# Four reorderings in a two-block transformer kernel on one core: copies before exps, one subtraction on another engine, one transpose later, one wait later

## The reference, cut to what matters

```python
mem_n = rms_norm(mem, mem_norm)
for i in range(2):
    hn = rms_norm(h, norm_pre[i])
    k_m, v_m = split(mem_n @ w_mem_kv[i])              # keys and values of the memory
    if i == 0:   # latent attention: q, k, v made from a 672-wide latent, with rope
        proj = hn @ w_in_a;  main = mla_mixer(...)     # 12 heads, causal softmax
    else:        # attention with cumulated forget gates added to the logits
        proj = hn @ w_in_b;  main = fox_mixer(...)     # 12 heads, causal softmax
    mem_out = memory_attention(q_m, k_m, v_m)          # 4 heads, softmax over 256 memory tokens
    y = concat([main, mem_out]) * silu(gate)
    h = h + rms_norm(y @ w_out[i], norm_post[i])
```

## Time and profile before

| what | value |
|---|---|
| three runs | 1202.85, 1203.97, 1208.3 us |
| profiled execution, its own time | 1202.74 us |
| span of its instructions | 1201.0 us |
| PE busy | 1179.9 us (98%) |
| ACT, DVE, POOL busy | 594.2, 534.2, 432.5 us |
| mean granted PE clock | 0.994 of full |

### The profile page before, as it was taken

The page is one execution under the profiler, slowest core; times in us unless marked ns, Lnnn a source line. Parts: engine busy times, 40 slices in busy tenths (PEclk is TensorE's granted clock), DMA queues, the critical chain, the costliest instruction groups (busy, mean ns, idle before and its releaser), DMA issues.

```text
span 1201.0 us, 16232 instructions
## 1 busy us (share of the span) xinstructions
PE 1179.9 (98%) x6127; PEld 915.8 (76%) x6127; DVE 534.2 (44%) x979; ACT 594.2 (49%) x1246; POOL 432.5 (36%) x261
## 2 busy tenths in 40 slices
PE   7999999999999999989999999999999999999998
PEld 7988855568988666658888987787666677888886
DVE  4211465644210555553476645601786760033333
ACT  7344666554343655564644654544565552333142
POOL 6534721214344222215344322344222223444451
PEclk9999999989999999989999999999999999999999
DMA  8533211202336999813222321233121213323221
GB/s 297 141 106 68 64 23 47 68 21 84 108 98 77 95 62 79 122 35 90 89 88 68 108 67 57 75 101 105 53 58 52 67 37 91 102 92 102 96 97 70
DMA packets 111550, 100.97 MB, mean 84 GB/s; under 512 B 21157, under 2 KB 98289, under 8 KB 111473
## 3 DMA queue, kind: packets, MB, share of 16 engines
q1 hardware_dynamic: 108928, 95.35, 33.8%
q0 software_dynamic: 864, 3.15, 0.7%
q10 hardware_dynamic: 1680, 1.44, 0.4%
HBM read 94.68 MB, written 2.10 MB: 81 GB/s over the span
## 4 chain that ended last, share of the span: by engine, by line
PE 94%; DVE 2%; ACT 2%; DMA 1%; issue 1%; POOL 1%; SPq 0%; DVEq 0%; ACTq 0%
PE bank L592 49%; PE bank L1936 8%; PE bank L1629 7%; PE bank L1423 6%; PE bank L861 4%; PE bank L879 3%; PE bank L895 3%; PE bank L1952 2%; PE bank L1250 2%; PE bank L1967 2%; PE bank L1979 2%; PE bank L865 1%; PE bank L1718 1%; DMA w_raw<-in_w_mem_kv 1%; PE bank L702 1%
## 5 line engine op out<-in xcount | busy, mean ns | idle before, releaser
L527 POOL TENSOR_TENSOR w_lo<-w_raw,w_hi 128x1024 fp32r<-128x1024 f32 (+5 forms) x159 | 358.7, 2256 | 695.3 <-ACT w_hi L512 695.3
L512 ACT ACTIVATE w_hi<-w_raw 128x1024 fp32r<-128x1024 f32 (+6 forms) x161 | 159.2, 989 | 229.6 <-PE bank L592 203.4
L592 PE MATMUL bank<-acts_hi,w_hi 128*128 128x512 f32 (+1 forms) x576 | 224.0, 389 | 0.9 <-POOL w_lo L527 0.9
L592 PE MATMUL bank<-acts_lo,w_hi 128*128 128x512 f32 (+1 forms) x576 | 222.6, 386 | 0.0
L592 PE MATMUL bank<-acts_hi,w_lo 128*128 128x512 f32 (+1 forms) x576 | 222.5, 386 | 0.0
L592 PEld LDWEIGHTS bank<-acts_hi,w_hi 128*128 128x128 f32 x576 | 108.1, 188 | 24.3 <-POOL w_lo L527 1.4
L592 PEld LDWEIGHTS bank<-acts_lo,w_hi 128*128 128x128 f32 x576 | 108.1, 188 | 22.1
L592 PEld LDWEIGHTS bank<-acts_hi,w_lo 128*128 128x128 f32 x576 | 108.2, 188 | 21.4
L2073 DVE TENSOR_TENSOR_SCAN arena_end<-arena 128x512 f32<-128x512 f32 (+3 forms) x64 | 83.8, 1309 | 60.3 <-ACT arena L2024 60.3
L592 PE MATMUL bank<-w_hi,acts_hi 128*128 128x512 f32 (+4 forms) x240 | 86.8, 362 | 0.1
L592 PE MATMUL bank<-w_hi,acts_lo 128*128 128x512 f32 (+4 forms) x240 | 86.2, 359 | 0.0
(11 more groups left out here) (301 smaller groups left out, 2122.6 us busy)
## 6 DMA issues: line engine op xcount, KB each, us to landing
w_raw<-in_w_in SPq DMA_DIRECT2D x64, 512.0 KB, 3.6
w_raw<-in_w_out SPq DMA_DIRECT2D x24, 512.0 KB, 3.6
w_raw<-in_w_in_b SPq DMA_DIRECT2D x22, 512.0 KB, 5.3
w_raw<-in_w_in_a SPq DMA_DIRECT2D x10, 512.0 KB, 3.9
w_raw<-in_w_mem_kv SPq DMA_DIRECT2D x8, 512.0 KB, 8.3
w_raw<-in_w_sb_proj SPq DMA_DIRECT2D x8, 512.0 KB, 3.4
w_raw<-in_w_ssd_proj SPq DMA_DIRECT2D x8, 512.0 KB, 3.4
arena_shared<-junk SPq DMA_DIRECT2D x11, 256.0 KB, 20.7
```

Source lines behind the costliest of these rows:

```text
L512: nc.scalar.activation(w_at(p)[0][:, 0:size], w_raw[p % RAW][:, 0:size], ACT.Copy).then_inc(w_high.sem, 1)
L527: nc.gpsimd.tensor_tensor(lo[:, 0:size], w_raw[p % RAW][:, 0:size], hi[:, 0:size].bitcast(F32), ALU.subtract).then_inc(w_rest.sem, 1)
L592: mm = nc.tensor.matmul(bank_of(S, s, g)[0:lhs.shape[1], 0:rhs.shape[1]], lhs, rhs, start=j + kk + t == 0, stop=j == len(S.pieces) - 1 and ...
```

## The change

Four edits, all of order:

1. **Copies ahead of exps**: in steps 28, 29 and 31 (before: 31 alone) of both sweeps ACT does `collect_w` before `exp`.
2. **A low part on DVE**: the low part of the second piece of `pA_out` and of `pB_out` is made by DVE at the end of its step 28 (`rest_dve`, L538 of the changed kernel), no longer by POOL.
3. **Second block of x turned later**: PE transposes block 1 after the first piece of `p_mem[1]`, no longer before it; ACT's copy of it comes after the high part of piece 5.
4. **First score of the second sweep sooner**: PE's waits for the last evacuation of the gate projection and for `gates_in` move from before step 0 to before the scores of step 1. To fit, `counts` gives step 0 nothing and step 1 sixteen matmuls of the q and k projection (before 8 and 8).

```diff
+        def rest_dve(dve, p):
+            hi, lo = w_at(p)
+            size = pieces[p][0] * pieces[p][1]
+            dve.wait_ge(w_high.sem, p + 1)
+            dve.wait_ge(w_rest.sem, p)
+            nc.vector.tensor_tensor(lo[:, 0:size], w_raw[p % RAW][:, 0:size], hi[:, 0:size].bitcast(F32),
+                                    ALU.subtract).then_inc(w_rest.sem, 1)
...
                     size = piece_size(S, k, q + 2)
+                    if S.piece0 + q + 2 in rest_on_dve:
+                        continue
                     if size:
+                        if S.piece0 + q + 1 in rest_on_dve:
+                            pool.wait_ge(w_rest.sem, S.piece0 + q + 2)
                         pool.wait_ge(w_high.sem, S.piece0 + q + 3 + S.turn * k)
...
+                for ready in second if s == 1 else ():
+                    pe.wait_ge(*ready)
...
+            copies_first = (steps - 4, steps - 3, steps - 1)
             for s in range(steps + lag):
-                if s == steps - 1:
+                if s in copies_first:
...
+                if s == last:
+                    rest_dve(dve, pA_out.piece0 + 1)
...
-                    return (8, 8, 8, 8, 8, 8, 5, 5)[s]
+                    return (0, 16, 8, 8, 8, 8, 5, 5)[s]
...
+        rest_on_dve.update(S.piece0 + 1 for S in (pA_out, pB_out))
...
             round_act(act, pre[0], 0)
-            round_act(act, pre[0], 1)
             split_ahead_act(act, p_mem[1], 0, 0)
             norm_act_step(act, pre[0], 2, x_in_sem, rounds=False)
             split_ahead_act(act, p_mem[1], 0, 1)
+            round_act(act, pre[0], 1)
             project_act(act, p_mem[1], split=2)
...
             norm_pe_step(pe, pre[0], 0)
-            norm_pe_step(pe, pre[0], 1)
-            project_pe(pe, p_mem[1])
+            project_pe(pe, p_mem[1], turns_in={(None, 0): (pre[0], 1)})
...
             project_pe(pe, pB_gate)
-            pe.wait_ge(*pB_gate.evac(2 * MB))
-            pe.wait_ge(sem["gates_in"], 1)
             fox_pe(pe)
```

More of the change, by code:

```diff
@@ L528, in rest @@
                                     ALU.subtract).then_inc(w_rest.sem, 1)
+        rest_on_dve = set()
+        def rest_dve(dve, p):
[5 more added lines that the diff above has]
+                                    ALU.subtract).then_inc(w_rest.sem, 1)
         def split_ahead_act(act, S, k, q):
@@ L843, in sweep_stage, with sweep_pe @@
                          C["gated_hi"].take(len(pairs)), C["gated_lo"].take(len(pairs)))
-        def sweep_pe(pe, A, turn_in, counts, beside=None, lag=1, bank_free=None, begin_next=None):
+        def sweep_pe(pe, A, turn_in, counts, beside=None, lag=1, bank_free=None, begin_next=None, second=()):
             steps = len(A.steps)
@@ L956, in sweep_act @@
                 between(s)
-                if s != steps - 1:
+                if s not in copies_first:
                     collect_w(2 * s - 2 * lag)
@@ L1434, in counts @@
                 return 0
-            sweep_pe(pe, attB, turn_in, counts, lag=2, begin_next=lambda j: begin_out(pe, pB_out, attB, j))
+            sweep_pe(pe, attB, turn_in, counts, lag=2, second=(pB_gate.evac(2 * MB), (sem["gates_in"], 1)), begin_next=lambda j: begin_out(pe, pB_out, attB, j))
         def fox_act(act):
@@ L1467, in after @@
                     dve.wait_ge(C["product"].sem, pB_qk.done_after(0, pB_qk.n - 1, 0))
+                if s == 4 * (MP + B_H // 2 - 1):
+                    rest_dve(dve, pB_out.piece0 + 1)
                 if s == 4 * (MP + B_H // 2 - 1) + 1:
```

## The result

The changed kernel takes 1192.51 us by the median of four runs (1192.23 to 1192.82); the kernel before takes 1206.13 by the median of its four beside them (1202.85 to 1208.89). The ratio of the two is 0.9898, with a 95% interval of 0.988 to 0.9916. The profiled execution took 1192.82 us, against 1202.74 before: 9.92 us less, where the prediction's sum was 10.1. The medians lie 13.6 us apart because two of the four executions before took 1208.3 and 1208.89 us, some 5 us more than the other two, so this text compares the profiled executions.

A forecast was written before the change was run, and what follows sets the result against it. PE, busy 98% of the span, bounds the kernel; only its waits and half-clock time can be won. 0.9 + 4.7 + 3.9 + 0.6 = 10.1 us off 1202.74 gives 1192.6, as a median 1193.8; range 1190.5 to 1199.5.

The forecast's parts named there:

- The clock: Ends of both sweeps: no more half clock, 0.44 us saved per busy us, 2.5 us in each sweep.
- Edits 1 and 2, first sweep: End of first sweep: earlier transposes and scores win 2.2 us, the clock staying up 2.5 us; 4.7 us in all.
- the 0.4 us for which PE was to wait for an exp: First sweep, ahead of the scores of step 30: some 0.4 us of idle time left.
- Second sweep: End of second sweep: 2.65 us of wait plus 2.5 of clock, less 1.3 for DVE's subtraction; 3.9 us.
- the term of 1.3 us: Second sweep: DVE's subtraction ahead of the maxima comes through as a 1.3 us wait before step 29's transposes.
- Edit 3: Start: PE's 1.18 us wait for DVE's scaling of block 1 goes; 0.9 us won, ends 0 and 1.2.
- The lower figure: Start: 0.6 us, not 0.9, if the port lock made block 2's scaling hold up piece 6's low part.
- Edit 4: Start of second sweep: the first score fills the 0.69 us wait; 0.6 us won, ends 0 and 0.7.
- the rule from the first part: From 534.8 to 1195 us PE is busy throughout, so what it gains ahead of that reaches the end.
- the clock falls all the same: Rival, second sweep: waits around step 29 bring half clock, costing 3.4 us; 1197.2 us, chance 0.21.
- the wait changes its name: Rival, both sweeps: delayed exps hold scores as copies held transposes, clock falls as before; 1202.5 us, chance 0.11.
- The slower case: Rival, both sweeps: DVE's 2.35 us subtraction delays step 30's maxima, clock drops a second time; 1210.2 us, chance 0.04.

The follow-up runs named there:

- Filling the waits alone: Kernel before with only 5 (first sweep) and 9 (second sweep) small matmuls put ahead of PE's waits for the copies of step 26: 1197.90 us median, 1197.63 profiled.
- edit 1 alone: Kernel before with only ACT's copies put ahead of the exps at steps 28 and 29: 1195.20 us median, 1194.59 profiled.
- edit 2 alone: Kernel before with only the low part of one piece moved from POOL to DVE at the end of both sweeps: 1197.78 us median, 1196.61 profiled.
- all but edit 2: Changed kernel with POOL making the low part as before: 1193.98 us median, 1194.13 profiled.
- the rows of f sooner: Changed kernel with SP issuing each pair's two row copies behind the even piece of weights, not the odd one: 1196.56 us median, 1196.72 profiled.
- edit 3 alone: Kernel before with only the second block of x turned later: 1201.57 us median, 1200.64 profiled.

## Why the prediction held, and the step that did not

**The clock, right.** Two falls at 2.5 us each were half of the sum. Filling the waits alone gave 5.1 us. The price of 0.44 us per busy us came from one form at both clocks, and stood. The rivals had 0.5 us per us and so 3.4 us for a fall, which is too much by the same measure.

**Edits 1 and 2, first sweep, right.** Worked out: transposes of step 27 at 239.2, scores of step 30 at 240.15, 4.7 us in all. Measured on the old time axis (add the 1.28 us by which PE came sooner): 239.25, 240.08, and 6.19 - 1.28 = 4.9 us. Of the 0.4 us for which PE was to wait for an exp, 0.17 us came, and only on the weight load's row: the last exp of step 28 ended at 238.62.

**Second sweep, right in sum, a term mis-sized.** 9.93 - 5.69 = 4.2 us against 3.9. The subtraction came at 1.22 us, as estimated from the earlier trace rows, and stands squarely ahead of the maxima, as said:

```profile
512.76 1.22 DVE L538 TENSOR_TENSOR w_lo<-w_raw,w_hi 128x1024 fp32r<-128x1024 f32 x1
...
514.89 0.62 ACT L951 ACTIVATE arena<-arena,stat 128x384 f32<-128x384 f32 x1 [0.47 <-DVE stat L989]
...
517.09 0.30 PE L895 MATMUL bank<-ident,arena 128*128 128x128 f32 x1 [0.59 <-ACT arena L962]
```

But of its 1.22 us only 0.59 reached PE, since 2.38 us of values and 1 us of scores lie between. I let the values count as cover in the first sweep and forgot them in the second. So the term of 1.3 us was some 0.7 too high. A part of that was eaten by a wait that the sum did not have, 0.20 us ahead of step 28's transposes (512.23), so the sweep came out only 0.3 us better than forecast.

**Edit 3, right.** 0.9 expected; alone it brought 0.93 us. The lower figure that the prediction had for this term, 0.6 us, did not come. In the changed kernel piece 2 starts at 19.71 with a wait of 0.21 us for its low part, `p_mem[2]` at 26.45 (said: 26.6), without the 0 to 0.4 us that POOL might have taken. Blocks 1 and 2 are transposed at 22.69 and 35.10 without a wait:

```profile
19.71 0.39 PE L606 MATMUL bank<-w_hi,acts_hi 128*128 128x256 f32 x1 [0.21 <-POOL w_lo L527]
```

**Edit 4, wrong.** "It fills the gap", 0.6 us, with the rule from the first part that what PE gains goes through to the end. That sentence was read from the stretch behind 534.8 us and is true there. For gains made ahead of 400 us it is not: from 400 to 496 us the DMA engines are 0.94 busy, a piece lands 22 us after its issue, and the even pieces were already just in time (one wait of ACT for 1.28 us in the kernel before). PE was 6.19 us ahead behind the first sweep and 7.07 by the third score of the second (398.55 before, 391.48 after), so edit 4 had won 0.88. The pieces landed only 4.8 to 5.6 us sooner than before, and 1.38 of these 7.07 us were lost by 514.67: waits of 0.57 and 0.43 us, and about 0.17 for each beyond its row. That is edit 4's 0.88 and 0.5 of the lead that it added to. The DMA share was a column of the stretches all along; I had read it for the ends of the sweeps and not for their middle.

By the table of leads the parts are 1.28 (start), 4.91 (first sweep), -0.50 (between) and 4.24 (second sweep), 9.93 in all; the sum had 0.9, 4.7, +0.6 and 3.9. Three terms came out 0.2 to 0.4 us above the forecast and hid one that was 1.1 below it, so that the sum met the profiled execution within 0.2 us is in part luck. Of the start's 1.28 us 0.26 is no edit's, since PE is that much ahead already at its first weights (12.43, before 12.69); this leaves 1.0 for edit 3. For the median the forecast was 1193.8 us, 1.2 above the sum, since the profiled execution before lay that much below its median; the changed kernel's executions lie close together, and its median came to 1192.51.

**Rivals.** That the clock falls all the same did not come, though by the mean clock it did in some executions with one of the two edits: one of seven with edit 1 alone (0.996), at least three of seven with edit 2 alone (0.995), and two of six with all but edit 2 (0.996). It was a fair rival. That the wait changes its name did come, but elsewhere: not exps for copies at the sweeps' ends, but DMAs in the middle. The slower case was far off, as its one mechanism (the subtraction ahead of the maxima) costs 0.59 us.

## What to carry to other kernels

Price idle time on a matmul engine twice: by itself, and by what the granted clock does behind it; fill it with idle matmuls to tell the two apart in one run. A gain goes through only as far as the next resource with a pace of its own, so read the DMA share and the issue-to-landing times of every stretch between the gain and the end, not only where PE waits now. And where one edit is enough in a good execution, a second can still be worth having for the margin.

## What the runs showed of the hardware

- **A row read 128 times from one partition is slow.** While such copies run alone the DMA view of the stretch shows 26 to 28 GB/s, and the two copies of a pair (256 KB each) land about 9 us apart, with the DMA engines counted as busy. Read from eight partitions, a pair and a 512 KB piece of weights, all issued from 408.16 us on, were done by 414.4 us. The Trainium skill, SBUF — State Buffer, section "Door 1: The DMA port swizzle", says that DMA bandwidth depends on how many of 16 ports the partitions reach, 435 GB/s in all. Its share for one port, 27 GB/s (an estimate from that page), is what the trace shows; the prediction didn't draw on it. SP's issue of a 512 KB piece behind such copies takes 6.9 us, and 0.37 us without them:

```profile
474.68 6.91 SPq L468 DMA_DIRECT2D w_raw<-in_w_out  x1
```

```profile
469.75 0.37 SPq L468 DMA_DIRECT2D w_raw<-in_w_out  x1
```

- **The clock fell behind short waits, and for two lengths.** It fell behind single waits of 1.54 and 2.65 us before, and of 1.68 us with edit 2 alone, for 6.83 or 3.41 us; it stayed up behind waits of 0.65 and 1.02 us in the profiled executions. The length of a wait does not decide alone: with the rows of f sooner it stayed up behind one of 1.77 us too, at 494.31 in the second sweep's middle, where PE was busy for 5.07 of 6.84 us, about as in the stretch of 6.65 us ahead of the first fall before (4.95). There the work ahead of the wait was mostly the q and k projection, with 512 columns to a matmul; ahead of the falls it was scores and transposes. What makes the difference, no run here shows.
- **Open.** The guess that the spread of the kernel before is the clock's holds only for its lower part. Of its 48 executions beside the experiments, 36 lie from 1199.4 to 1203.9 us, the lowest at a mean clock of 0.998, the highest at 0.993 or 0.994; 12 lie from 1205.0 to 1208.3, with the same 0.993 to 0.995. These carry some 4 us that the clock doesn't account for, as do two executions with edit 1 alone (1199.8 and 1200.7) and two with edit 3 alone. There is no trace of any of them. With both edits, and with filled waits, no execution did this (47 in all), and I can't say why.
